# RWKV chunk loop on one core: fill products in eight runs in place of thirteen, and 32-row products that alternate between two tiles

## The reference

```python
def step(state, inp):
    r_t, w_t, k_t, v_t, kk_t, a_t = inp
    sa = jnp.einsum('bhij,bhj->bhi', state, -kk_t)
    state = (state * w_t[:, :, None, :]
             + sa[..., None] * (kk_t * a_t)[:, :, None, :]
             + v_t[..., None] * k_t[:, :, None, :])
    y_t = jnp.einsum('bhij,bhj->bhi', state, r_t)
    return state, y_t
```

## Time and profile before

| | |
|---|---|
| median of 3 runs | 885.13 us |
| lowest and highest | 884.59 and 888.14 us |
| profiled execution, its own time | 885.59 us |
| its span in the profile | 883.9 us |
| PE busy | 850.9 us (96%) |
| DVE, ACT, POOL busy | 411.5, 334.4, 118.6 us |
| granted TensorE clock, mean | 0.995 of full |
| chain that ended last, by engine | PE 87%, DVE 8%, ACT 3%, issue 1% |

### The profile page before, as it was taken

How to read it: one execution, slowest core, us unless ns; L and a number is a source line. 1 busy time by engine, 2 the same in 40 slices (tenths; PEclk the granted TensorE clock), 3 DMA queues, 4 the chain that set the end, 5 groups by cost and what they waited for, 6 DMA issues and landing times.

```text
span 883.9 us, 12041 instructions
## 1 busy us (share of the span) xinstructions
PE 850.9 (96%) x4561; PEld 670.5 (76%) x4561; DVE 411.5 (47%) x600; ACT 334.4 (38%) x512; POOL 118.6 (13%) x124
## 2 busy tenths in 40 slices
PE   5999999999999999999999899999999999999995
PEld 4677767778778677667888688888888888888884
DVE  5379677443452544544662464444444444222214
ACT  6568241322323533334431364444444444211122
POOL 3054850220222301100330000000000000000000
PEclk9999999999999999999999999999999999999998
DMA  6421441320115222122334233333333332222222
GB/s 199 121 72 49 108 130 45 88 72 14 37 37 166 73 73 70 50 72 72 95 133 158 67 95 95 95 95 95 95 95 95 96 104 95 102 90 90 92 70 95
DMA packets 122298, 79.45 MB, mean 90 GB/s; under 512 B 15033, under 2 KB 110322, under 8 KB 122258
## 3 DMA queue, kind: packets, MB, share of 16 engines
q1 hardware_dynamic: 122066, 78.87, 30.1%
q0 software_dynamic: 192, 0.02, 0.0%
HBM read 73.63 MB, written 5.24 MB: 89 GB/s over the span
## 4 chain that ended last, share of the span: by engine, by line
PE 87%; DVE 8%; ACT 3%; issue 1%; DMA 0%; POOL 0%; SPq 0%; ACTq 0%; DVEq 0%
PE PS L1483 25%; PE PS L1484 24%; PE PS L1485 24%; PE PS L1835 1%; PE PS L1579 1%; DVE sq L1175 1%; DVE w_lo L1101 1%; PE PS L1846 1%; PE PS L1684 1%; DVE gates L1376 1%; PE PS L1724 1%; PE PS L1723 1%; PE PS L1702 1%; PE PS L1762 1%; PE PS L1594 1%
## 5 line engine op out<-in xcount | busy, mean ns | idle before, releaser
L1483 PE MATMUL PS<-hT_hi,w_hi 128*128 128x512 f32 (+1 forms) x664 | 269.5, 406 | 8.7 <-DVE gates L1376 3.9
L1485 PE MATMUL PS<-hT_hi,w_lo 128*128 128x512 f32 (+1 forms) x664 | 259.9, 391 | 0.0
L1484 PE MATMUL PS<-hT_lo,w_hi 128*128 128x512 f32 (+1 forms) x664 | 259.6, 391 | 0.0
L1101 DVE TENSOR_TENSOR w_lo<-wraw,w_hi 128x1024 fp32r<-128x1024 f32 (+1 forms) x125 | 164.9, 1320 | 161.1 <-ACT w_hi L763 159.4
L763 ACT ACTIVATE w_hi<-wraw 128x1024 fp32r<-128x1024 f32 (+1 forms) x125 | 131.3, 1050 | 139.1 <-PE PS L1485 113.9
L1483 PEld LDWEIGHTS PS<-hT_hi,w_hi 128*128 128x128 f32 (+1 forms) x664 | 124.4, 187 | 44.8 <-issue 17.4
L1485 PEld LDWEIGHTS PS<-hT_hi,w_lo 128*128 128x128 f32 (+1 forms) x664 | 124.4, 187 | 27.4
L1484 PEld LDWEIGHTS PS<-hT_lo,w_hi 128*128 128x128 f32 (+1 forms) x664 | 124.7, 188 | 24.6 <-issue 1.0
L1484 PE MATMUL PS<-w_lo,act_hi 128*128 128x512 f32 x176 | 70.3, 399 | 0.0
L1483 PE MATMUL PS<-w_hi,act_hi 128*128 128x512 f32 x176 | 69.4, 394 | 0.0
L1485 PE MATMUL PS<-w_hi,act_lo 128*128 128x512 f32 x176 | 69.0, 392 | 0.0
(11 more groups left out here) (237 smaller groups left out, 1044.6 us busy)
## 6 DMA issues: line engine op xcount, KB each, us to landing
wraw<-in_w_ffn_in_dram SPq DMA_DIRECT2D x88, 256.0 KB, 3.1
wraw<-in_w_in_dram SPq DMA_DIRECT2D x82, 256.0 KB, 3.3
wraw<-in_w_ffn_out_dram SPq DMA_DIRECT2D x44, 256.0 KB, 2.9
wraw<-in_w_o_dram SPq DMA_DIRECT2D x16, 256.0 KB, 3.0
xt<-in_x_dram SPq DMA_DIRECT2D x4, 512.0 KB, 4.9
qk_scratch<-stage SPq DMA_DIRECT2D x8, 256.0 KB, 3.0
qkT<-qk_scratch SPq DMA_DIRECT2D x4, 512.0 KB, 4.8
wraw<-in_w_up_a_dram SPq DMA_DIRECT2D x8, 256.0 KB, 3.1
```

Source lines behind the costliest of these rows:

```text
L1101: dve.tensor_tensor(w_lo[:, q, 0:n], wraw[:, s, 0:n], w_hi[:, q, 0:n].bitcast(F32), ALU.subtract)\
L1483: pe.matmul(out_, a_hi, b_hi, start=start, stop=False)
L1484: pe.matmul(out_, a_hi, b_lo, start=False, stop=False)
L1485: return pe.matmul(out_, a_lo, b_hi, start=False, stop=stop)
```

## The change

On TensorE the parts of the fill units are put into fewer runs: in chunks 1 to 3 the run ahead of the scores keeps parts 0 and 1, parts 2 to 5 stand in one run between score pairs 2 and 4, parts 6 and 7 come between the scores and `tokens`. In chunk 0 the scores had six parts ahead of them and none between; now they have three and three. Of the second unit the parts go 2 (after `products_32`), 2 (after `merge_32`), 1 (after `products_64`), 1 (in `solve`), 2 (ahead of `state`), in place of 1, 1, 1, 1, 1, 2, 1. No fill part stands between `state` and `outputs` any more. Chunks 0 to 3 had 9, 13, 13 and 12 runs (in the last chunk no `state` divides the last two) and have 8, 8, 8 and 8.

`products_32` and `merge_32` were called once for each half, with all heads of a half in a row; now one call goes over the heads and issues both halves of a head next to each other. On ACT `fill_out` of the first unit stands ahead of `tokens`.

```diff
                 split_hi(U_QK + 2 * c + LEAD, U_QK + 2 * c + LEAD)
+                fill_out(2 * c)
                 tokens(c)
-                fill_out(2 * c)
...
-                fill(c, 0, 0, 2 if c else 6)
+                fill(c, 0, 0, 2 if c else 3)
...
-                    if c:
-                        fill(c, 0, 2 + q // 2, 1)
+                    if q == 2:
+                        fill(c, 0, *((2, 4) if c else (3, 3)))
...
-            def products_32(c, half):
+            def products_32(c):
...
+                pe.wait_ge(score_ready, 8 * c + 4)
...
+                    pe.wait_ge(G_ready, 2 * c)
                 for h in range(NH):
-                    ins = pe.matmul(PS[hi, 4 + half, QB * h:QB * h + QB], MT_rb[lo, h, 0, hi], Tc[lo, h % 4, h // 4, c, :],
-                                    start=True, stop=True, tile_position=(HD * half, HD * half + QB))
-                ins.then_inc(pr_mm, 1)
+                    for half in range(2):
+                        lo, hi = slice(HD * half, HD * half + QB), slice(HD * half + QB, HD * half + HD)
+                        ins = pe.matmul(PS[hi, 4 + half, QB * h:QB * h + QB], MT_rb[lo, h, 0, hi],
+                                        Tc[lo, h % 4, h // 4, c, :], start=True, stop=True,
+                                        tile_position=(HD * half, HD * half + QB))
+                        if h == NH - 1:
+                            ins.then_inc(pr_mm, 1)
...
-            def merge_32(c, half):
+            def merge_32(c):
...
+                pe.wait_ge(pr_ready, 4 * c + 2)
                 if c:
-                    pe.wait_ge(U_ready, 2 * (c - 1) + half + 1)
+                    pe.wait_ge(U_ready, 2 * c)
                 else:
                     pe.wait_ge(m_odd_ready, NP_)
-                if half:
-                    pe.wait_ge(fill_ready, 2 * c + 1)
+                pe.wait_ge(fill_ready, 2 * c + 1)
                 for h in range(NH):
...
+                    for half in range(2):
...
+                        if half == 0:
+                            pe.matmul(PS[hi, 6, QB * h:QB * h + QB], tt, w, start=True, stop=True,
+                                      tile_position=(QB, QB))
+                        ins = pe.matmul(PS[lo, 6 + half, 256 + QB * h:256 + QB * h + QB], w, tt,
+                                        start=True, stop=True, tile_position=(HD * half + QB, HD * half))
+                        if h == NH - 1:
+                            ins.then_inc(zz_mm, 1)
...
-                fill(c, 1, 4, 1)
+                fill(c, 1, 5, 1)
...
                 scores(c)
+                fill(c, 0, 6, 2)
                 tokens(c)
-                fill(c, 0, 6, 2)
                 if c:
                     y_T(c - 1)
-                products_32(c, 0)
-                fill(c, 1, 0, 1)
-                products_32(c, 1)
-                fill(c, 1, 1, 1)
-                merge_32(c, 0)
-                merge_32(c, 1)
-                fill(c, 1, 2, 1)
+                products_32(c)
+                fill(c, 1, 0, 2)
+                merge_32(c)
+                fill(c, 1, 2, 2)
                 products_64(c, 0)
                 products_64(c, 1)
-                fill(c, 1, 3, 1)
+                fill(c, 1, 4, 1)
                 merge_64(c, 0)
                 merge_64(c, 1)
                 solve(c)
-                fill(c, 1, 5, 2)
+                fill(c, 1, 6, 2)
                 if more:
                     state(c)
-                fill(c, 1, 7, 1)
                 outputs(c)
```

More of the change, by code:

```diff
@@ L1595, in tokens @@
                     ins.then_inc(tok_mm, 1)
-            def products_32(c, half):
[L1599 to L1610, removed]
-                for h in range(NH):
-                    ins = pe.matmul(PS[hi, 4 + half, QB * h:QB * h + QB], MT_rb[lo, h, 0, hi], Tc[lo, h % 4, h // 4, c, :],
-                                    start=True, stop=True, tile_position=(HD * half, HD * half + QB))
-                ins.then_inc(pr_mm, 1)
+            def products_32(c):
+                pe.wait_ge(score_ready, 8 * c + 4)
+                if c == 0:
+                    pe.wait_ge(t_loaded, 16 * NQ)
+                    pe.wait_ge(TTc_ready, 1)
+                    pe.wait_ge(vb_ready, TT)
+                    pe.wait_ge(bonv_ready, NP_)
+                else:
+                    pe.wait_ge(yc_ready, c)
+                    pe.wait_ge(G_ready, 2 * c)
+                for h in range(NH):
+                    for half in range(2):
[5 more added lines that the diff above has]
+                            ins.then_inc(pr_mm, 1)
             def products_64(c, half):
@@ L1623, in products_64 @@
                 ins.then_inc(pr_mm, 1)
-            def merge_32(c, half):
-                lo, hi = slice(HD * half, HD * half + QB), slice(HD * half + QB, HD * half + HD)
-                pe.wait_ge(pr_ready, 4 * c + half + 1)
+            def merge_32(c):
+                pe.wait_ge(pr_ready, 4 * c + 2)
                 if c:
-                    pe.wait_ge(U_ready, 2 * (c - 1) + half + 1)
+                    pe.wait_ge(U_ready, 2 * c)
                 else:
                     pe.wait_ge(m_odd_ready, NP_)
-                if half:
-                    pe.wait_ge(fill_ready, 2 * c + 1)
+                pe.wait_ge(fill_ready, 2 * c + 1)
                 for h in range(NH):
[L1636 to L1643, removed]
+                    for half in range(2):
+                        lo, hi = slice(HD * half, HD * half + QB), slice(HD * half + QB, HD * half + HD)
+                        w = PR[hi, h // 4, h % 4, 0:QB]
+                        tt = TTc[hi, h % 4, h // 4, c, :]
+                        if half == 0:
[5 more added lines that the diff above has]
+                            ins.then_inc(zz_mm, 1)
             def merge_64(c, half):
```

## The result

The changed kernel takes 875.69 us (median of 4 runs, 874.29 to 876.74) where the kernel before takes 886.60 (median of 4 runs by now, 884.59 to 888.14): a ratio of 0.988, 95% interval 0.9856 to 0.9905. That is 10.9 us less; 10.8 was forecast. The profiled execution took 876.74 us, with a span of 875.0. The forecast started from 885.13 us, the median of the three executions then known; a fourth moved it to 886.60.

The account below looks back on a forecast made before the run. PE's own stream was taken to set the length of a chunk. Savings of 2.74 + 2.60 + 2.93 + 2.52 = 10.8 us took the median from 885.13 to 874.3 us, own range 873 to 876; 872.8 to 879.3 holds 0.8.

Parts of the forecast that it names:

- (a): Scores: two cuts fewer and part 5's own run gone; 1.00 us saved in each of chunks 1 to 3.
- (b): Score pairs 4 and 6: masked copies free the banks in time, ending the stall; 0.33 us in chunk 2.
- (c): `tokens` takes about 1.17 us in place of 1.46; 0.29 saved in chunks 1 and 2, nothing in chunk 3.
- (d): `products_32`: alternating halves take 0.63 us in place of 1.22; 0.59 saved a chunk, bounds 0.11 and 0.65.
- (e): `merge_32`: the third tile overlaps, block 0.65 us in place of 1.03; 0.38 saved, bounds 0 and 0.43.
- The rival of no overlap: `products_32` and `merge_32`: records of the two halves go one after another; 877.3 us, chance 0.14.
- the one of a drain at each step: `products_32` and `merge_32`: PE drains on every step between the halves' tiles; slower, 900 us, chance 0.05.
- the estimate of 878 us: Whole time if a 25 ns floor limited alternation in `products_32` to about 0.3 us a chunk, `merge_32` losing as much.
- (f): Second unit: four one-part runs become two of two; 0.34 us saved, 0.24 if leaving `state` costs `outputs`; chunk 3: 0.22.
- (g): ACT's `fill_out` ahead of `tokens`: 0.60 us before the token copies, covered by 0.4; uncovered, 0.2 to 0.6 a chunk.
- The rival of waits in place of the cuts: At `tokens` and the second unit, longer runs cover less often, each chunk losing 1 us; 878.3 us, chance 0.08.
- Given back later: Attention part: weight transfers or ACT set its length, so half the gain is lost; 880 to 881 us, chance 0.05.

Follow-up runs that it names:

- x4_one_more_run: Changed kernel with one fill part moved between score pairs 0 and 2, one more run a chunk; 877.38 us, ratio 0.9903.
- x8_fourth_tile: Changed kernel with a fourth product per head, at tile (96, 96), added to the merges; 876.5 us (one execution).
- x1_halves_apart: Changed kernel with `products_32` and `merge_32` issued half by half again, fill runs kept; 879.83 us, ratio 0.9939.
- x6_cover_gone: Changed kernel with no fill between 64-row products and merges, that part joining the run behind `merge_32`; 874.96 us, ratio 0.9867.
- x5_copy_out_late: Changed kernel with ACT's `fill_out` of the first unit behind `tokens` again; 878.46 us (one execution).

## Why the prediction was right, point by point

The forecast was 10.8 us in the chunks; the chunk sum fell by 10.08. By chunk: 2.74, 2.60, 2.93, 2.52 forecast, 2.54, 2.37, 2.69, 2.48 found. The whole time fell by 10.9, which agrees with both within its interval (8.4 to 12.8 us). That it meets the forecast to 0.1 is luck: the chunks fell 0.7 short of it, the profiled spans differ by 8.9, and the medians come from four executions that scatter by 2.5 to 3.6 us. The mechanism is what was right, term by term, as follows.

**(a), cost of a run**: 0.40 us, confirmed by the added runs of x4_one_more_run (1.60 us for four). Starts of chunk 2 were forecast as 1.59, 3.53, 6.51 and 8.45 us after its beginning; they are 1.59, 3.51, 6.50 and 8.43.

**(b), banks free in time**: right. DVE's masked copies in chunk 2 start 4.38 us after the chunk (4.37 forecast):

```profile
215.84 2.58 DVE L1222 COPY_PREDICATED MT_rb<-m_si,PS 128x512 f32<-128x512 uint32 x4
...
219.13 2.60 DVE L1222 COPY_PREDICATED LK_rk<-m_si,PS 128x512 f32<-128x512 uint32 x4 [0.71 <-PE PS L1579]
```

and pair 4 waits for nothing.

**(c), tokens**: mechanism right, size off. Three sets take 1.30 us (221.41 to 222.71), not 1.17: they run 0.43 to 0.44 each, back to back. The wait for the eighth copy is gone. 0.13 us lost in chunks 1 and 2.

**(d) and (e), alternation**: 0.63 us for the products, as forecast; 0.63 for the merges where 0.65 was. That the third tile rides along was a reading of how half 1's records began before half 0's had ended; x8_fourth_tile shows that a fourth does too. The rival of no overlap and the one of a drain at each step both fall with the row of x32. The lower bound of (d), 0.11 us for one change of arrangement less, was too small: x1_halves_apart takes 1.02 where two blocks of 0.61 stood, 0.20 less. In the traces 48 records start within 0.53 us (0.63 less the 0.10 to leave), 11 ns each, and 64 in 0.58, 9 ns each; on the same tile it is 31 ns from record to record. The Trainium skill (TensorE: Matmul & The Clock Gate, Part 1, "Wait — 56ns, not 53.3ns?") states that start-to-start never drops below about 25 ns. The trace disagrees with it for products that alternate between tiles (11 and 9 ns), and the estimate of 878 us falls with it.

**(f), the second unit's runs**: the gap between `state` and `outputs` gave nothing. `outputs` takes 4.75 us (238.87 to 243.62) where it took 4.65 (246.77 to 251.42): the cost of leaving `state` moved into it, the bound of 0.24 that was named. The other part of this step, that the covers were needed as they stood, was wrong in one place: behind the 64-row products no cover was needed, as x6_cover_gone shows, so the change left 0.1 us a chunk lying there; the 0.44 that chunk 0 gains in that run comes from the joins.

**(g), ACT's order**: covered, and no effect either way (x5_copy_out_late). The rival of waits in place of the cuts falls with it: no wait stands at `tokens` or behind it in chunks 1 to 3.

**Chunk 0**: 2.54 in place of 2.74. PE starts the 32-row products 0.21 us behind the end of the blocks' transpose, not 0.05:

```profile
159.27 1.22 DVE L1207 STREAM_TRANSPOSE TTc<-Tc 128x1024 f32<-128x1024 f32 x1
```

ends at 160.49, the products start at 160.70. POOL's first instruction stands as far behind it in both kernels (161.20 to 161.41 before), so the row to take it from was at hand. The wait for the joins came, at 0.28 us for 0.4 forecast. The 0.1 us at `outputs` is missing here too, as in chunks 1 and 2.

**Given back later**: nothing was in the attention part; the stretches behind the chunks have the same waits (gate copies 3.9 us in 11 pieces). But the prediction named a longer stretch behind the chunks as a sign of being wrong, and by its letter that sign came: 600.1 us before, 601.5 after. The 1.4 us are the second transposes (5.21 us where they took 3.84) at the lower clock, in a part that the change doesn't touch, and the sign didn't allow for that.

## What to carry to other kernels

Filler work that hides waits has a price of its own: here each run laid between two score products of one kind cost 0.40 us beside its work, read as the difference between starts with and without it and confirmed by adding one. Set each filler against the wait that it truly covers, and read that wait by the first half that the next step needs, not by the block of both. Small products of different tiles should stand next to each other in the stream; but when both halves then end together, the engine behind them starts later, and the filler behind must grow.

Where one region of a trace repeats to 0.1 us and whole runs scatter by 3, compare the region, and read its steps too: one trace in fourteen had a stray 0.7 us in it. A total that agrees with a theory doesn't yet show it: in x6_cover_gone the sum fitted and its parts didn't.

## What the runs showed of the hardware that was not expected

Records of 32 x 32 products on three or four different tiles start 11 and 9 ns apart on average, with 31 ns between two on the same tile; adding a fourth tile to three cost 0.05 us for 16 records.

An idle stretch of 3.35 us of TensorE in front of 32 transposes left them at 5.2 to 6.6 us in eleven of twelve profiled kernels without added matmuls in it (3.84 in the other), and 3.84 and 3.85 us where 2.92 us of matmuls filled it. The granted clock was 0.50 over the first of them in the changed kernel.

A VectorE transpose of 128 x 1024 elements let PE and POOL start 0.21 us after its recorded end (160.49 to 160.70 in the changed kernel).
